# Five buffers for gathered U rows and three for gathered V rows in a product-key expert layer, in place of four and four

## The chip, the cores and the metric

The kernel runs on one core of a Trainium2 chip. The metric is device time in microseconds (us) from launch to end, the median of several executions. The profile is of one execution; its span is the time from the first instruction to the last.

## What is computed

One layer of a decoder for 1024 prompt tokens and 32 sample tokens (8 sequences of 4), model width 1024, all in float32: a modulated norm and one combined projection, sliding-window attention, a gated short convolution, the output projection, and then a feed-forward layer (PEER) that takes most of the time. Cut to that layer, the reference is:

```
q = (xb @ w_query)                      # 8 heads, 2 halves of 64
s = einsum('thcd,hcnd->thcn', q, keys)  # 128 keys in each half
sv, si = top_k(s, 16)                   # 16 best of each half
cv, ci = top_k(all 256 sums, 16)        # 16 best pairs
idx = i1 * 128 + i2                     # one of 16384 experts
g = softmax(cv)
a = gelu(einsum('thkd,td->thk', expert_u[idx], xb))
out = einsum('thk,thkd->td', g * a, expert_v[idx])
```

Each token has 8 heads with 16 experts each; each expert has one row of 1024 numbers (4 KB) in `expert_u` and one in `expert_v`.

## The kernel before, in words

The program has four stages that end in a barrier of all engines (modulation rows; attention of the prompt; attention of the sample; the first half of the convolution) and then the long last one, from about 1050 us to the end. It does the expert layer, and beside it the second half of the convolution's 80 weight blocks (`conv_steps`), the output projection and the queries of the later token tiles (`out_steps`).

The expert layer goes by *units*. A unit is one tile of 128 tokens and one head: 8 tiles by 8 heads are 64 units, and the sample tokens are 2 more, `UNITS` = 66. A unit has 16 steps `k`, one for each chosen expert of a token; `at = n * 16 + k` numbers the steps of all units, 0 to 1055. In each step:

- GpSimd (POOL) issues two indirect DMAs. `gather_u(n, k)` brings 128 rows of `expert_u`, one to each partition (512 KB), into a buffer of `u_ring`. `gather_v(n - 1, k)` does the same from `expert_v` for the unit before, into a buffer of `v_ring`. All 2112 go through one DMA queue, in the order U, V, U, V, and POOL does nothing else in this stage.
- VectorE (DVE) multiplies the U rows with the tokens and sums (`dot_rows`, L1247, "dot" below): one number for each token. A dot signals `dots_done`. Between the dots stand the top-16 searches for the next unit (`pick_half`, `pick_best`, `pick_key`, `pick_index`), which give the indices `idx` that the next unit's gathers wait for (`idx_made`, after the dot of k = 12).
- After the 16 dots of a unit ScalarE (ACT) takes the GELU, DVE multiplies by the gates (`weigh`, after the first dot of the next unit), and ACT makes a 128x128 diagonal matrix of the weights for each step (`make_diag`, eight buffers).
- TensorE (PE) multiplies the diagonal with the V rows (`add_row`, L1574, "block" below): two products of 128x512 in float32, four MATMUL rows in the trace, accumulated in two banks over the 128 steps of a tile. A block signals `rows_done`.

Each ring has `RING` = 4 buffers of 1024 words in each partition. U gather number `at` waits until the dot of number `at - 4` has released its buffer, V gather `at` until the block of number `at - 4` has:

```python
for n in range(UNITS + 1):
    if n < UNITS:
        pool.wait_ge(idx_made, n + 1)
    for k in range(TOPK):
        if n < UNITS:
            gather_u(n, k)
        if n:
            gather_v(n - 1, k)
```

Since POOL works in order, a V gather that waits for its buffer also holds back the U gathers behind it, and the reverse. At the end, for the last unit, only V gathers are left. After every 8 units DVE multiplies the summed banks out (`finish_y`), and PE's first block of the next tile waits for that.

Of the kernel before, what the change touches and what calls it, by code (L numbers as in the profile page):

```python
# [15 lines left out]
D = 1024  # L16
# [17 lines left out]
LOWEST = -3.0e38  # L34
PH, PK, TOPK = 8, 128, 16
UNITS = NT * PH + 2
RING = 4
DIAGS = 8
IDXS = 4
ABLK = 512  # L40
# [18 lines left out]
def build(nc, x_prompt, x_sample, cache_k, cache_v, state_conv, c_prompt, c_sample,  # L59
# [17 lines left out]
    eu = expert_u.rearrange("a n d -> (a n) d")  # L77
    ev = expert_v.rearrange("a n d -> (a n) d")
# [10 lines left out]
    with ctx:  # L89
# [3 lines left out]
        def sem(name):  # L93
            return ctx.enter_context(nc.semaphore(name))
# [19 lines left out]
        def row(names, at, *shape, dt=F32):  # L114
            n = 1
            for s in shape:
                n *= s
            n = (n + 7) // 8 * 8
            return [place(name, at + i * n, *shape, dt=dt) for i, name in enumerate(names)]
# [3 lines left out]
        def banks(a, n):  # L123
            return bank[:, a:a + n, :].rearrange("p a b -> p (a b)")
# [106 lines left out]
        def merged_T(j, k):  # L231
            if j < HT:
                return oT1[:, k, j * P:j * P + P]
            if j < NT:
# [1 line left out]
            return oT2[:, k, NP - NA:NBT]  # L236


        u_ring = row([f"u_ring{r}" for r in range(RING)], 0, D)
        v_ring = row([f"v_ring{r}" for r in range(RING)], 4096, D)  # L240
        h2b = row(["h2b0", "h2b1"], 8192, D)
        x2_now, y_now = row(["x2_now", "y_now"], 10240, D)
        prod = row(["prod0", "prod1"], 12288, D)
        G2 = place("G2", 14336, D)
        diag = row([f"diag{r}" for r in range(DIAGS)], 15360, P)
# [49 lines left out]
        q0_ps = sem("q0_in_psum")  # L295
        e_consts, e_keys_ps, e_keys_made, e_g2_in = (sem(n) for n in (
            "e_consts", "keys_in_psum", "keys_made", "g2_in"))
        u_in = [sem(f"u_in_{r}") for r in range(RING)]
        v_in = [sem(f"v_in_{r}") for r in range(RING)]
        q_in = [sem(f"q_in_{r}") for r in range(2)]  # L300
        dots_done, rows_done, s_ps, s_out, best_made, gate_exp, idx_made, gelu_made, wgt_made, diag_made = (
            sem(n) for n in ("dots_done", "rows_done", "s_in_psum", "s_out", "best_made", "gate_exp",
                             "idx_made", "gelu_made", "wgt_made", "diag_made"))
# [166 lines left out]
        @block.gpsimd  # L470
        def _(pool):
            link = Chain(pool, chain_pool)

            def where(view, pattern, base, mult, cmp, fill):
                link(pool.affine_select(out=view, in_=view, compare_op=cmp, fill=fill, base=base,
                                        pattern=pattern, channel_multiplier=mult))

            link(pool.memset(ident[:, :], 0.0))
            where(ident[:, :], [[-1, P]], 0, 1, ALU.not_equal, 1.0)
            link(pool.memset(sel_s[:, :], 0.0))  # L480
            for q in range(4):
                where(sel_s[:, :], [[-1, NS]], -NS * q, 1, ALU.not_equal, 1.0)
            link(pool.memset(eps[:, :], EPS))
            pool.sem_inc(consts_made, 1)
            barrier(pool, 0)

            link(pool.memset(maskt[:, :, :, :], 0.0))
            for m, own in ((0, 0), (1, 1), (2, 0)):
                where(maskt[:, m, own, :], [[-1, P]], 0, 1, ALU.is_ge, NEG)
                if m:  # L490
                    where(maskt[:, m, 1 - own, :], [[1, P]], -1, -1, ALU.is_ge, NEG)
            link(pool.memset(maskt[:, 0, 1, :], NEG))
            link(pool.memset(kpad[:, :, :, :, :], 0.0))
            link(pool.memset(vpad[:, :, :, :], 0.0))
            pool.sem_inc(attn_zeroed, 1)
            for t in range(NT):
                pool.wait_ge(qkv_out, t + 1)
                if t:
                    pool.wait_ge(pv_ps, t * 4)
                for half in range(2):  # L500
                    link(pool.tensor_copy(vpad[:, t % 2, :, 2 * HD * half:2 * HD * half + HD],  # L501
                                          qkv[:, D + KVW:QKV].rearrange("p (g d) -> p g d", g=NKV)))
                pool.sem_inc(v_placed, 1)
            barrier(pool, 1)

            link(pool.memset(s_mask[:, :], 0.0))
            link(pool.memset(qz[:, :, :, :, :], 0.0))
            cache = s_mask[0:NS, 0:NB * WIN].rearrange("p (b j) -> p b j", b=NB)
            new = s_mask[0:NS, NB * WIN:].rearrange("p (b l) -> p b l", b=NB)
            where(cache, [[-L, NB], [0, WIN]], 0, 1, ALU.is_ge, NEG)  # L510
            where(cache, [[L, NB], [0, WIN]], L - 1, -1, ALU.is_ge, NEG)
            where(cache, [[L, NB], [1, WIN]], -1, -1, ALU.is_ge, NEG)
            where(new, [[-L, NB], [0, L]], 0, 1, ALU.is_ge, NEG)
            where(new, [[L, NB], [0, L]], L - 1, -1, ALU.is_ge, NEG)
            where(new, [[-L, NB], [-1, L]], 0, 1, ALU.is_ge, NEG)
            pool.sem_inc(mask_s_made, 1)
            barrier(pool, 2)
            link(pool.iota(part_i[:, :], pattern=[[1, TOPK]], base=0, channel_multiplier=0))
            link(pool.tensor_copy(iota16[:, :], part_i[:, :]))
            link(pool.memset(keys_bd[:, :, :], 0.0))  # L520
            pool.sem_inc(e_consts, 1)
            barrier(pool, 3)

            def gather_u(n, k):
                at = n * TOPK + k
                if at >= RING:
                    pool.wait_ge(dots_done, at - RING + 1)
                pool.indirect_dma_start(out=u_ring[k % RING][:, :], out_offset=None, in_=eu,  # L528
                                        in_offset=bass.IndirectOffsetOnAxis(ap=idx[n % IDXS][:, k:k + 1], axis=0)
                                        ).then_inc(u_in[k % RING], 16)  # L530

            def gather_v(n, k):
                at = n * TOPK + k
                if at >= RING:
                    pool.wait_ge(rows_done, at - RING + 1)
                pool.indirect_dma_start(out=v_ring[k % RING][:, :], out_offset=None, in_=ev,  # L536
                                        in_offset=bass.IndirectOffsetOnAxis(ap=idx[n % IDXS][:, k:k + 1], axis=0)
                                        ).then_inc(v_in[k % RING], 16)

            for n in range(UNITS + 1):  # L540
                if n < UNITS:
# [6 lines that stand above are left out]
# [334 lines left out]
        def _(dve):  # L882
            link = Chain(dve, chain_dve)
            V = nc.vector
            w = dve.wait_ge
# [353 lines left out]

            def dot_rows(n, k):  # L1240
                at, t = n * TOPK + k, n // PH
                w(u_in[k % RING], 16 * (at // RING + 1))
                if at >= 2:
                    w(dots_done, at - 1)
                if at % (PH * TOPK) == 0 and t:
                    w(h2_in, 16 * t if t < NT else 16 * (NT + 3))
                V.tensor_tensor_reduce(out=prod[k % 2][:, :], in0=u_ring[k % RING][:, :],  # L1247
                                       in1=h2b[t % 2][:, :], scale=1.0, scalar=0.0, op0=ALU.mult,
                                       op1=ALU.add, accum_out=dot[n % 2][:, k:k + 1]).then_inc(dots_done, 1)

# [87 lines left out]
        def _(pe):  # L1338
            M, TR = nc.tensor.matmul, nc.tensor.transpose
            w = pe.wait_ge  # L1340
# [4 lines left out]
            for rows, n, at in ((c9, NB + 1, 0), (st16, NB * 2, 72), (cw4, 4, 200)):  # L1345
                for k in range(KC):
                    last = TR(small[:, at + k * n:at + (k + 1) * n], rows[0:n, k * P:(k + 1) * P], ident[0:n, 0:n])
            last.then_inc(small_ps, 1)
            pe.wait_ge(small_made, 1)
            for j in range(NBLK):  # L1350
                r = j % ARING
# [3 lines left out]
                for k in range(KC):  # L1355
                    last = M(banks(r, 1)[0:NB + 1, :], cT[:, k, :], ada_w[r][:, k, :], start=k == 0, stop=k == KC - 1)  # L1356
# [116 lines left out]
            for c in range(2):  # L1473
                for b in range(NB):
                    last = TR(banks(3 + 2 * c, 2)[:, b * P:(b + 1) * P], ck_sb[:, b, c * P:(c + 1) * P], ident[:, :])
# [90 lines left out]
            def add_row(n, k):  # L1566
                at, parts = n * TOPK + k, P if n < NT * PH else NS
                first, final = at % (PH * TOPK) == 0, (at + 1) % (PH * TOPK) == 0 or at + 1 == UNITS * TOPK
                if first and at:
                    w(y_read, n // PH)  # L1570
                w(v_in[k % RING], 16 * (at // RING + 1))
                w(diag_made, at + 1)
                for c in range(2):
                    last = M(banks(c, 1)[0:parts, :], diag[k % DIAGS][:, 0:parts], v_ring[k % RING][:, c * 512:(c + 1) * 512],  # L1574
                             start=first, stop=final)
                last.then_inc(rows_done, 1)

# [84 lines left out]
```

## Time and profile before

| | us |
|---|---|
| median of 3 runs | 4266.62 |
| lowest and highest of the runs | 4257.82, 4269.5 |
| the profiled execution's own time | 4249.22 |
| its span | 4247.4 |

| engine | busy us | share of the span |
|---|---|---|
| PE (matmul) | 3373.3 | 79% |
| DVE | 2463.8 | 58% |
| POOL | 2427.2 | 57% |
| ACT | 1004.3 | 24% |

The page reports 1259.02 MB moved by DMA, 1107.43 MB of them by the queue that POOL's gathers use. An issue of a gather counts as busy time of POOL, from its start until POOL can go on. "To landing" is the time from the start of that issue to the last of the 16 semaphore updates of the transfer. A released buffer shows as an idle time of POOL "<-PE bank L1574" (V) or "<-DVE dot L1247" (U) in front of a gather; 0.30 us of idle time stand in front of every gather, whether it waited or not.

### The profile page before, as it was taken

How to read it: one execution, taken by the hardware profiler on the slowest of the kernel's cores; microseconds unless marked ns; L12 is line 12 of the kernel's file. 1: busy time of each engine (PE TensorE's matmuls, PEld its weight loads, DVE VectorE, ACT ScalarE, POOL GpSimd, SP SyncE). 2: the span in 40 equal slices, each digit the busy share in tenths (PEclk: the TensorE clock that was granted, in tenths of full speed). 3: DMA queues.
4: the chain of work that ended last, by engine and by line, in shares of the span. 5: the costliest groups of instructions: out<-in, count | busy, mean ns of one | idle time of the engine just before them, and what ended most of it. 6: DMA issues, size and time to landing. Idle time of an engine off the chain costs nothing.

```text
span 4247.4 us, 35040 instructions
## 1 busy us (share of the span) xinstructions
PE 3373.3 (79%) x10326; PEld 1700.1 (40%) x10326; DVE 2463.8 (58%) x5652; ACT 1004.3 (24%) x2229; POOL 2427.2 (57%) x2160
## 2 busy tenths in 40 slices
PE   8577774997797899989998777776787677778777
PEld 1244443784443455545554332332242233223221
DVE  1244443344665677777676666666666666666663
ACT  0244442221122222222222221212121212222221
POOL 0000000001676777777776677777777777777776
PEclk9788896998899999999999999999999999999999
DMA  8100001643899999999999999999999999999998
GB/s 294 49 10 10 0 8 40 194 136 114 325 380 381 378 367 379 375 365 392 361 369 368 389 360 373 364 367 360 370 368 366 364 364 355 370 378 362 359 371 322
DMA packets 439469, 1259.02 MB, mean 296 GB/s; under 512 B 41209, under 2 KB 142265, under 8 KB 438696
## 3 DMA queue, kind: packets, MB, share of 16 engines
q0 software_dynamic: 304128, 1107.43, 69.3%
q1 hardware_dynamic: 114700, 131.24, 9.3%
q10 hardware_dynamic: 20454, 18.13, 1.4%
q8 instruction: 85, 1.39, 0.1%
q14 instruction: 102, 0.84, 0.1%
HBM read 1233.67 MB, written 25.00 MB: 296 GB/s over the span
## 4 chain that ended last, share of the span: by engine, by line
PE 35%; POOL 23%; DMA 23%; issue 10%; DVE 6%; ACT 2%; ACTq 0%; DVEq 0%; SPq 0%; POOLq 0%
DMA v_ring<-in_expert_v_dram,idx 19%; PE bank L1574 13%; POOL u_ring L528 12%; POOL v_ring L536 11%; PE bank L1503 7%; PE bank L1371 4%; DMA u_ring<-in_expert_u_dram,idx 3%; PE bank L1356 2%; PE bank L1530 2%; PE bank L1406 2%; PE bank L1549 1%; PE bank L1384 1%; DVE prod L1247 1%; PE bank L1392 1%; PE bank L1595 1%
## 5 line engine op out<-in xcount | busy, mean ns | idle before, releaser
L1574 PE MATMUL bank<-v_ring,diag 128*128 128x512 f32 (+1 forms) x4224 | 2079.9, 622 | 603.3 <-DMA v_ring<-in_expert_v_dram,idx 486.1
L1247 DVE CUSTOM_DVE_ANT_0 prod<-u_ring,h2b 128x1024 f32<-128x1024 f32 x1056 | 1288.5, 1226 | 972.6 <-DMA u_ring<-in_expert_u_dram,idx 884.9
L528 POOL DMA_INDIRECT u_ring<-in_expert_u_dram,idx x1056 | 1197.0, 1134 | 649.0 <-issue 307.4
L536 POOL DMA_INDIRECT v_ring<-in_expert_v_dram,idx x1056 | 1207.7, 1144 | 430.5 <-issue 228.0
L1574 PEld LDWEIGHTS bank<-v_ring,diag 128*128 128x128 f32 (+1 forms) x4224 | 744.2, 191 | 1758.2 <-DMA v_ring<-in_expert_v_dram,idx 1034.0
L810 ACT ACTIVATE diag<-ident,wgt 128x128 f32<-128x128 f32 x1024 | 352.5, 393 | 781.0 <-PE bank L1574 519.2
L1503 PE MATMUL bank<-hi,whi 128*128 128x512 f32 x640 | 315.7, 493 | 8.2 <-DVE wlo L1108 8.2
L501 POOL COPY vpad<-qkv 128x256 f32<-128x256 f32 x16 | 7.5, 467 | 459.1 <-PE bank L1406 420.1
L1503 PE MATMUL bank<-hi,wlo 128*128 128x512 f32 x640 | 251.7, 393 | 0.0
L1503 PE MATMUL bank<-lo,whi 128*128 128x512 f32 x640 | 251.6, 393 | 0.0
L802 ACT ACTIVATE act_dot<-dot 128x16 f32<-128x16 f32 x66 | 14.2, 216 | 816.8 <-DVE dot L1247 816.7
L1371 PE MATMUL bank<-w_qkv,hT 128*128 128x512 f32 x384 | 169.0, 597 | 1.1 <-ACTq L579 1.1
L1549 PEld LDWEIGHTS bank<-mT,wq_sb 128*128 128x128 f32 x1152 | 138.8, 192 | 30.7 <-issue 30.6
L711 ACT CAST whi<-wc 128x1024 fp32r<-128x1024 f32 x80 | 83.8, 1048 | 278.3 <-PE bank L1595 174.1
L1503 PEld LDWEIGHTS bank<-hi,whi 128*128 128x128 f32 x640 | 121.7, 190 | 65.1 <-issue 43.7
L1108 DVE TENSOR_TENSOR wlo<-wc,whi 128x1024 fp32r<-128x1024 f32 x80 | 98.0, 1225 | 82.5 <-ACT whi L711 78.4
L1503 PEld LDWEIGHTS bank<-lo,whi 128*128 128x128 f32 x640 | 121.8, 190 | 56.1 <-issue 36.2
L1530 PE MATMUL bank<-wo_sb,oT 128*128 128x512 f32 (+1 forms) x288 | 136.7, 606 | 8.5 <-ACTq L769 6.0
L1549 PE MATMUL bank<-mT,wq_sb 128*128 128x128 f32 (+1 forms) x1152 | 138.5, 274 | 0.0
L1503 PEld LDWEIGHTS bank<-hi,wlo 128*128 128x128 f32 x640 | 120.9, 189 | 27.1
L1406 PE MATMUL bank<-pT,vpad 128*128 128x128 f32 x512 | 80.8, 324 | 48.1 <-issue 32.9
L1371 PEld LDWEIGHTS bank<-w_qkv,hT 128*128 128x128 f32 x384 | 73.0, 192 | 90.5 <-issue 88.8
(223 smaller groups left out, 2663.5 us busy)
## 6 DMA issues: line engine op xcount, KB each, us to landing
wc<-in_w_in_dram SPq DMA_DIRECT2D x80, 512.0 KB, 7.7
ada_w<-in_w_ada_dram SPq DMA_DIRECT2D x12, 2048.0 KB, 8.0
u_ring<-in_expert_u_dram,idx POOLq DMA_INDIRECT x1056, 6.5
v_ring<-in_expert_v_dram,idx POOLq DMA_INDIRECT x1056, 6.5
wo_sb<-in_w_out_dram SPq DMA_DIRECT2D x2, 4096.0 KB, 18.8
wq_sb<-in_w_query_dram SPq DMA_DIRECT2D x2, 4096.0 KB, 19.3
w_qkv<-in_w_in_dram SPq DMA_DIRECT2D x1, 6144.0 KB, 22.9
q_st<-q_dh ACTq DMA_DIRECT2D x65, 64.0 KB, 5.4
```

Of the source, the lines that this page charges most:

```text
L528: pool.indirect_dma_start(out=u_ring[k % RING][:, :], out_offset=None, in_=eu, in_offset=bass.IndirectOffsetOnAxis(ap=idx[n % IDXS][:, k:k ...
L536: pool.indirect_dma_start(out=v_ring[k % RING][:, :], out_offset=None, in_=ev, in_offset=bass.IndirectOffsetOnAxis(ap=idx[n % IDXS][:, k:k ...
L810: nc.scalar.activation(diag[k % DIAGS][:, 0:parts], base[:, :], ACT.Copy, scale=wgt[n % 2][:, k:k + 1]).then_inc(diag_made, 1)
L1108: V.tensor_tensor(wlo[b % 2][:, :, :], wc[b % WRING][:, :, :], whi[b % 2][:, :, :].bitcast(F32), ALU.subtract).then_inc(w_split, 1)
L1247: V.tensor_tensor_reduce(out=prod[k % 2][:, :], in0=u_ring[k % RING][:, :], in1=h2b[t % 2][:, :], scale=1.0, scalar=0.0, op0=ALU.mult, op1 ...
L1356: last = M(banks(r, 1)[0:NB + 1, :], cT[:, k, :], ada_w[r][:, k, :], start=k == 0, stop=k == KC - 1)
L1371: last = M(banks(c, 1), hT(t)[:, k, :], w_qkv[:, k, c * 512:(c + 1) * 512], start=k == 0, stop=k == KC - 1)
L1406: last = M(banks(7, 1)[:, at:at + P], vpad[:, s, g, HD * e:HD * e + P], pT[:, s, 2 * pair + e, :], start=e == 0 and s == 0, stop=e == 1 an ...
L1503: last = M(at, (wlo if part == 2 else whi)[b % 2][:, k, :], (lo if part == 1 else hi)[:, k, 0:NA], start=(k, part) == (0, 0), stop=(k, par ...
L1530: last = M(banks(2 + c, 1)[0:parts, :], merged_T(j, k), wo_sb[:, k, c * 512:(c + 1) * 512], start=k == 0, stop=k == KC - 1)
L1549: last = M(banks(2, 2)[:, h * P:h * P + parts], wq_sb[:, k, h * P:(h + 1) * P], mT[:, k, 0:parts], start=k == 0, stop=k == KC - 1)
L1574: last = M(banks(c, 1)[0:parts, :], diag[k % DIAGS][:, 0:parts], v_ring[k % RING][:, c * 512:(c + 1) * 512], start=first, stop=final)
```

## The change

`RING` is replaced by `URING` = 5 and `VRING` = 3. The eight buffers take the same 8192 words in each partition: U the first 5120, V the next 3072. U gather `at` now waits for the dot of number `at - 5`, V gather `at` for the block of number `at - 3`. The buffer and its semaphore are picked by `at` modulo the ring's size, where `k` modulo 4 did it before. Each engine's instructions stay the same in kind, number and order.

```diff
-RING = 4
+URING, VRING = 5, 3
...
-        u_ring = row([f"u_ring{r}" for r in range(RING)], 0, D)
-        v_ring = row([f"v_ring{r}" for r in range(RING)], 4096, D)
+        u_ring = row([f"u_ring{r}" for r in range(URING)], 0, D)
+        v_ring = row([f"v_ring{r}" for r in range(VRING)], URING * D, D)
...
             def gather_u(n, k):
                 at = n * TOPK + k
-                if at >= RING:
-                    pool.wait_ge(dots_done, at - RING + 1)
-                pool.indirect_dma_start(out=u_ring[k % RING][:, :], out_offset=None, in_=eu,
+                if at >= URING:
+                    pool.wait_ge(dots_done, at - URING + 1)
+                pool.indirect_dma_start(out=u_ring[at % URING][:, :], out_offset=None, in_=eu,
...
             def gather_v(n, k):
                 at = n * TOPK + k
-                if at >= RING:
-                    pool.wait_ge(rows_done, at - RING + 1)
-                pool.indirect_dma_start(out=v_ring[k % RING][:, :], out_offset=None, in_=ev,
+                if at >= VRING:
+                    pool.wait_ge(rows_done, at - VRING + 1)
+                pool.indirect_dma_start(out=v_ring[at % VRING][:, :], out_offset=None, in_=ev,
...
-                w(u_in[k % RING], 16 * (at // RING + 1))
+                w(u_in[at % URING], 16 * (at // URING + 1))
...
-                w(v_in[k % RING], 16 * (at // RING + 1))
+                w(v_in[at % VRING], 16 * (at // VRING + 1))
```

## Rows read from the trace of the kernel before

**Rows 1.** The page's chain that ended last: shares by engine, then by line.

```profile
PE 35%; POOL 23%; DMA 23%; issue 10%; DVE 6%; ACT 2%; ACTq 0%; DVEq 0%; SPq 0%; POOLq 0%
DMA v_ring<-in_expert_v_dram,idx 19%; PE bank L1574 13%; POOL u_ring L528 12%; POOL v_ring L536 11%; PE bank L1503 7%; PE bank L1371 4%; DMA u_ring<-in_expert_u_dram,idx 3%; PE bank L1356 2%; PE bank L1530 2%; PE bank L1406 2%; PE bank L1549 1%; PE bank L1384 1%; DVE prod L1247 1%; PE bank L1392 1%; PE bank L1595 1%
```

**Rows 2.** Busy time by stretch of the last stage; the first line names the columns.

```profile
core 0: us, PE busy (x) PEld busy (x) DVE busy (x) ACT busy (x) POOL busy (x), PEclk, DMA share, GB/s
1067.00:1260.00 193.00, 167.78 (x576) 89.94 (x577) 121.06 (x291) 42.41 (x93) 137.37 (x122) 0.93 0.95 352
1260.00:2230.00 970.00, 874.11 (x2894) 485.30 (x2894) 676.43 (x1611) 246.82 (x523) 727.29 (x631) 0.99 1.00 374
2230.00:4205.00 1975.00, 1502.32 (x3738) 612.90 (x3736) 1251.49 (x3049) 400.98 (x950) 1505.11 (x1328) 0.98 0.98 367
4205.00:4242.00 37.00, 34.10 (x77) 7.50 (x76) 3.43 (x7) 4.59 (x17) 15.69 (x17) 1.00 0.80 269
```

**Rows 3.** Timeline, DVE and POOL: start us, us, instruction, idle before, releaser.

```profile
3006.16 1.23 DVE L1247 CUSTOM_DVE_ANT_0 prod<-u_ring,h2b 128x1024 f32<-128x1024 f32 x1 [1.01 <-DMA u_ring<-in_expert_u_dram,idx]
3006.26 1.94 POOL L536 DMA_INDIRECT v_ring<-in_expert_v_dram,idx  x1 [0.30 <-issue]
...
3055.09 0.94 POOL L536 DMA_INDIRECT v_ring<-in_expert_v_dram,idx  x1 [0.30 <-issue]
3056.33 0.93 POOL L528 DMA_INDIRECT u_ring<-in_expert_u_dram,idx  x1 [0.30 <-issue]
3057.57 0.94 POOL L536 DMA_INDIRECT v_ring<-in_expert_v_dram,idx  x1 [0.30 <-issue]
```

**Rows 4.** V gathers of 1067 to 1260, 1260 to 2230, 2230 to 4205 us.

```profile
L536 POOL DMA_INDIRECT v_ring<-in_expert_v_dram,idx x61: 932/945/1967, 1067.4 to 1258.1; - x61
DMA to landing us min/median/max: 4.5/6.4/10.6
...
L536 POOL DMA_INDIRECT v_ring<-in_expert_v_dram,idx x315: 932/940/1979, 1261.2 to 2227.6; - x158
DMA to landing us min/median/max: 4.8/7.2/19.5
...
L536 POOL DMA_INDIRECT v_ring<-in_expert_v_dram,idx x664: 932/941/1979, 2230.5 to 4204.3; - x166
DMA to landing us min/median/max: 4.5/6.3/18.3
```

**Rows 5.** Waits of POOL in the same three stretches: us in total, times, longest.

```profile
POOL v_ring L536 <- PE bank L1574: 20.4, 20, 8.8
POOL u_ring L528 <- DVE dot L1247: 5.1, 3, 2.2
...
POOL v_ring L536 <- PE bank L1574: 48.4, 68, 8.1
POOL u_ring L528 <- DVE dot L1247: 21.6, 15, 4.2
...
POOL v_ring L536 <- PE bank L1574: 118.4, 221, 4.0
POOL u_ring L528 <- DVE dot L1247: 17.0, 18, 1.6
```

**Rows 6.** Timeline, first and last V gather counted, block third before each.

```profile
1077.90 3.75 PE L1574 MATMUL bank<-v_ring,diag 128*128 128x512 f32 x4 [23.52 <-ACT diag L810]
1078.28 1.63 POOL L536 DMA_INDIRECT v_ring<-in_expert_v_dram,idx  x1 [0.31 <-issue]
...
4203.31 1.90 PE L1574 MATMUL bank<-v_ring,diag 128*32 128x512 f32 x4 [0.65 <-DMA v_ring<-in_expert_v_dram,idx]
4204.34 0.94 POOL L536 DMA_INDIRECT v_ring<-in_expert_v_dram,idx  x1 [0.30 <-issue]
```

**Rows 7.** The last unit, 4205 to 4242 us: V gathers alone.

```profile
DMA to landing us min/median/max: 4.8/5.2/6.6
...
4205.59 1.01 POOL L536 DMA_INDIRECT v_ring<-in_expert_v_dram,idx  x1 [0.30 <-PE bank L1574]
4235.13 0.94 POOL L536 DMA_INDIRECT v_ring<-in_expert_v_dram,idx  x1 [0.78 <-PE bank L1574]
```

More of the change, by code:

```diff
@@ L297, in build @@
             "e_consts", "keys_in_psum", "keys_made", "g2_in"))
-        u_in = [sem(f"u_in_{r}") for r in range(RING)]
-        v_in = [sem(f"v_in_{r}") for r in range(RING)]
+        u_in = [sem(f"u_in_{r}") for r in range(URING)]
+        v_in = [sem(f"v_in_{r}") for r in range(VRING)]
         q_in = [sem(f"q_in_{r}") for r in range(2)]
@@ L525, in gather_u @@
                 at = n * TOPK + k
-                if at >= RING:
-                    pool.wait_ge(dots_done, at - RING + 1)
-                pool.indirect_dma_start(out=u_ring[k % RING][:, :], out_offset=None, in_=eu,
+                if at >= URING:
+                    pool.wait_ge(dots_done, at - URING + 1)
+                pool.indirect_dma_start(out=u_ring[at % URING][:, :], out_offset=None, in_=eu,
                                         in_offset=bass.IndirectOffsetOnAxis(ap=idx[n % IDXS][:, k:k + 1], axis=0)
-                                        ).then_inc(u_in[k % RING], 16)
+                                        ).then_inc(u_in[at % URING], 16)
             def gather_v(n, k):
                 at = n * TOPK + k
-                if at >= RING:
-                    pool.wait_ge(rows_done, at - RING + 1)
-                pool.indirect_dma_start(out=v_ring[k % RING][:, :], out_offset=None, in_=ev,
+                if at >= VRING:
+                    pool.wait_ge(rows_done, at - VRING + 1)
+                pool.indirect_dma_start(out=v_ring[at % VRING][:, :], out_offset=None, in_=ev,
                                         in_offset=bass.IndirectOffsetOnAxis(ap=idx[n % IDXS][:, k:k + 1], axis=0)
-                                        ).then_inc(v_in[k % RING], 16)
+                                        ).then_inc(v_in[at % VRING], 16)
             for n in range(UNITS + 1):
@@ L1246, in dot_rows @@
                     w(h2_in, 16 * t if t < NT else 16 * (NT + 3))
-                V.tensor_tensor_reduce(out=prod[k % 2][:, :], in0=u_ring[k % RING][:, :],
+                V.tensor_tensor_reduce(out=prod[k % 2][:, :], in0=u_ring[at % URING][:, :],
                                        in1=h2b[t % 2][:, :], scale=1.0, scalar=0.0, op0=ALU.mult,
@@ L1570, in add_row @@
                     w(y_read, n // PH)
-                w(v_in[k % RING], 16 * (at // RING + 1))
+                w(v_in[at % VRING], 16 * (at // VRING + 1))
                 w(diag_made, at + 1)
                 for c in range(2):
-                    last = M(banks(c, 1)[0:parts, :], diag[k % DIAGS][:, 0:parts], v_ring[k % RING][:, c * 512:(c + 1) * 512],
+                    last = M(banks(c, 1)[0:parts, :], diag[k % DIAGS][:, 0:parts], v_ring[at % VRING][:, c * 512:(c + 1) * 512],
                              start=first, stop=final)
```

## The prediction

> **What bounds the kernel now.** I read the chain that ended last first. It names no single engine: V gathers in flight, the blocks that use them, and POOL's issues of both kinds of gather follow one another, 55% of the span between them [rows 1]. That is a loop through a buffer. Then busy time by stretch [rows 2]. From 1260 to 4205 us the DMA engines are busy 0.98 to 1.00 of the time at 367 to 374 GB/s. POOL is nearly full too: in the long stretch 1505.11 us of busy time and 1328 times the 0.30 us that stand before every gather make 1904 of 1975 us. The waits of POOL tell how little the rings hold it back [rows 5]: in that stretch V gathers waited 118.4 us in 221 cases, 52 us without the 0.30 us of each, U gathers 17.0 us in 18 cases. So today the DMA engines and POOL's issuing set the pace together, and four buffers of each kind are just enough to keep both going. One step takes 1975 / 664 = 2.97 us there and 970 / 315 = 3.08 us from 1260 to 2230 us [rows 2, 4]. When nothing disturbs it, POOL could issue a pair every 2.48 us [rows 3].
>
> **The change, part by part.** No instruction is added. Only two waits move.
>
> *The V side.* A V buffer's cycle is 0.30 us from release to issue, the time to landing, and the block of 1.90 us [rows 6]. With the median landing that is 0.30 + 6.3 + 1.90 = 8.5 us in the long stretch and 0.30 + 7.2 + 1.90 = 9.4 us in the one before [rows 4]. Four buffers gave it 4 x 2.97 = 11.9 and 4 x 3.08 = 12.3 us. Three give 8.9 and 9.2 us. The median gather just fits in the long stretch and just doesn't in the other. What costs time is the gathers over the median and the blocks that PE starts late, since it has convolution, projection and score products between them.
>
> I took each V gather's issue and the end of the block third before it, which will release its buffer after the change. The first of them started at 1078.28 us, and its block ended at 1077.90 + 3.75 = 1081.65: it would have had to wait 3.6 us more, with 0.28 us from release to issue. The last started at 4204.34 with its block ending at 4205.21: 1.1 us more [rows 6]. Of the 1040 V gathers between 1067 and 4205 us, 714 were issued before that moment. The lateness sums to 121 us over the first 61, 484 us over the 315 of the next stretch and 546 us over the 664 of the long one, 1151 us together.
>
> How much becomes time? Not the sum itself. When POOL stops for a V gather, all later gathers shift with it, and so the next two gathers don't have that wait again; the blocks that release them are old enough not to shift. Each wait counts three times in my sum, so the high end is 1151 / 3 = 384 us, if every gather takes as long to land as before. The low end is nothing: a stop of POOL lets the queue in front of the DMA engines drain, and gathers then land sooner. The rows have a stretch where the queue is short. In the last unit V gathers go alone, DMA is at 0.80, and they land in 5.2 us [rows 2, 7]. I take that as what a gather needs without a queue, so the cushions are 6.4 - 5.2 = 1.2 us in the first stretch, 7.2 - 5.2 = 2.0 in the second, 6.3 - 5.2 = 1.1 in the long one [rows 4, 7]. Only lateness above the cushion leaves DMA engines idle. Summed over the same gathers it is 64, 87 and 224 us, 375 together, and a third of it is **+125 us**. This is the value I take; 0 and 384 stay as its ends.
>
> The Trainium skill, "DMA: Bandwidth & Descriptors", section on the anatomy of one DMA, speaks against a loss of this size: it fits 2.0 us plus the bytes over 436 GB/s to a single DMA from GpSimd, an estimate of 3.2 us for 512 KB. With 3.2 us in place of 5.2 the cushions would be 3.2, 4.0 and 3.1 us, the lateness above them 11 + 15 + 42 = 68 us, and the term +23 us. No gather in these stretches landed in under 4.5 us, so the rows decide.
>
> *The last unit.* Its V gathers already wait for the ring each time: 15 intervals in 4235.13 - 4205.59 = 29.54 us, 1.97 us each, a four-buffer cycle of 7.9 us [rows 7]. Three buffers make 2.63 us of it, 15 x 0.66 = **+10 us**. Nothing covers this; both ends are close, since here all terms of the cycle stay.
>
> *The U side.* With a fifth buffer the waits of U gathers for a dot should go: 5.1 + 21.6 + 17.0 = 43.7 us in 36 cases, 33 us beyond the 0.30 us of each [rows 5]. While they lasted the DMA engines had a queue, so I count a third, as for V: **-11 us**, ends 0 and -33. The rest of the fifth buffer buys nothing. POOL reaches each U gather after the V gather in front of it, and that one is now the later. At a unit's start the fifth buffer also frees too early: its dot is number k = 11, but the indices come after the dot of k = 12.
>
> *POOL's issue time* is not fixed. It is 0.94 us in the median and up to 1.98 [rows 4]; the long ones start while a dot is running, and those are 1.23 us long [rows 3]. Moved issues may meet more or fewer dots. I price that at nothing, with 1.04 us for each issue that changes sides as the unit of the error; 40 net changes would be 40 us either way, part of the range.
>
> The sum is 125 + 10 - 11 = **+124 us**. Against the profiled execution it is 4249.2 + 124 = 4373 us. That execution is 17 us below the median of the runs, so I forecast 4266.6 + 124 = **4391 us**, 2.9% slower.
>
> **The rivals.**
>
> *Hidden by the DMA engines, no change.* The DMA share is 0.98 to 1.00 and the bytes are the same. The mean lateness for each gather is 484 / 315 = 1.5 and 546 / 664 = 0.8 us, each under its cushion of 2.0 and 1.1. If lateness were even, the V term would be 0, the sum 10 - 11, and the time 4266 us. Against it: it is not even, the longest landing is 18.3 to 19.5 us [rows 4] and 221 ring waits show up in a ring that is 3.4 us longer than the median cycle [rows 5]. Chance 0.07. The same Trainium skill page, in its section on bandwidth, would make this the outcome, since it puts the limit of HBM transfers at about 358 GB/s per core: a kernel at that limit doesn't feel its rings. The rows run at 367 and 374 GB/s over long stretches, above it.
>
> *Faster.* The U ring is the one that matters: its 33 us of waits go whole, and the V side costs only its last unit. That gives 4266.6 - 33 + 10 = 4244 us. It needs V gathers to land in under 3 x 2.97 - 2.20 = 6.7 us in the long stretch and 3 x 3.08 - 2.20 = 7.0 us in the other nearly always. The second median is already 7.2. Chance 0.03.
>
> *No cushion.* The landing time is transfer and reply, not queue; a drained queue shortens nothing. Then the V term is 384 us and the time 4266.6 + 384 + 10 - 11 = 4650 us. For it: gathers under 5 us are rare. Against it: the last unit's 5.2 us. Chance 0.06.
>
> *The change isn't there.* The rings could be so placed that U and V still meet as before. The waits in the diff say otherwise; it has no chance worth naming.
>
> **How the numbers follow.** The forecast has 0.84, the rivals 0.07, 0.03 and 0.06. A measurement of this kernel can tell about 0.3%, 13 us, from no change. Within the forecast the V term may be off by half of itself, because the cushion rests on one row and a third is the share only if lateness is spread evenly: +62 to about +190 us, with 10 - 11 and some 20 us for POOL's issue times around it. That is 4310 to 4480 us, and it leaves out the rivals and the forecast's own tails, 2 in 10. Faster gets the 0.03, no change its 0.07 and 0.01 of the forecast's lower tail, slower the rest.
>
> **What would show it.** V gathers waiting for PE should rise from 187 us [rows 5] in the three stretches to several hundred, with most gathers among them. U gathers should hardly wait for dots. Landing medians should fall, to between 5.2 and 6.0 us in the long stretch. The DMA share should drop to about 0.95 with the GB/s. POOL's busy time should stay near 2400 us. The last unit should take about 10 us more. I'd be wrong in kind if the V waits rose and the DMA share stayed at 0.98 (the first rival), wrong in size if landing stayed at 6.3 us and the time went past 4500 (the third).

## The result and the profile after

| | before, us | after, us |
|---|---|---|
| median | 4266.65 | 4488.28 |
| lowest, highest | 4257.82, 4269.5 | 4471.43, 4496.09 |
| profiled execution, its span | 4249.22, 4247.4 | 4486.26, 4484.4 |

The ratio is 1.0518, with a 95% interval of 1.0484 to 1.0552: the change costs 222 us, where I had forecast 124 and a range up to 4480. The sign and the place were right, and the size was not. One of six executions of the run v3_fill_one, further down, took 8309.75 us; its ratio leaves that one out, its median counts it.

The chain that ended last answers to [rows 1]. V gathers in flight rose from 19 to 28%, and POOL's two issues fell from 23 to 15%:

```profile
PE 38%; DMA 31%; POOL 15%; issue 7%; DVE 5%; ACT 2%; ACTq 0%; DVEq 0%; SPq 0%; POOLq 0%
DMA v_ring<-in_expert_v_dram,idx 28%; PE bank L1574 16%; POOL u_ring L528 8%; POOL v_ring L536 7%; PE bank L1503 7%; PE bank L1371 4%; DMA u_ring<-in_expert_u_dram,idx 2%; PE bank L1356 2%; PE bank L1406 1%; PE bank L1530 1%; PE bank L1549 1%; PE bank L1595 1%; PE bank L1384 1%; PE bank L1392 1%; DVE prod L1247 1%
```

The busy time by stretch answers to [rows 2]. The stretches are cut at the same gathers as there: V gathers 0 to 60, 61 to 375, 376 to 1039, and the last 16.

```profile
1071.50:1278.80 207.30, 171.44 (x578) 89.48 (x578) 123.31 (x293) 42.52 (x93) 132.59 (x122) 0.94 0.91 330
1278.80:2340.40 1061.60, 899.42 (x2894) 493.24 (x2894) 676.19 (x1610) 247.29 (x523) 704.93 (x631) 0.96 0.94 341
2340.40:4437.00 2096.60, 1537.53 (x3738) 621.65 (x3738) 1253.49 (x3049) 401.72 (x950) 1490.59 (x1327) 0.96 0.95 346
4437.00:4479.40 42.40, 33.90 (x72) 6.58 (x72) 1.75 (x5) 4.59 (x17) 15.35 (x16) 1.00 0.67 215
```

Cut at those gathers, the four stretches took 193.8, 969.3, 1975.1 and 36.8 us before. They grew by 13, 92, 122 and 6 us, which with 4 us ahead of them is the whole difference of the spans. Nothing is lost elsewhere. The DMA share fell to 0.94 and 0.95 and the bytes in a second with it, from 374 and 367 to 341 and 346 GB/s. TensorE's granted clock fell too, from 0.99 and 0.98 to 0.96 in both long stretches.

POOL's waits in the first three stretches answer to [rows 5]:

```profile
POOL v_ring L536 <- PE bank L1574: 44.2, 29, 10.9
...
POOL v_ring L536 <- PE bank L1574: 211.5, 157, 11.8
...
POOL v_ring L536 <- PE bank L1574: 302.8, 342, 5.7
```

V gathers waited 558.5 us in 528 cases, against 187.2 us in 309 before. Without the 0.30 us of each that is 400 us against 94. No row of a U gather that waits for a dot is left, where there were 33 us net. POOL's busy time went down by 43 us, from 2427.2 to 2383.9. 306 - 33 - 43 = 230 us accounts for nearly all of the 237 us between the spans. That is POOL's own time line added up: it says where the time appears, not yet why.

The landing times answer to [rows 4], in the same three stretches, and the last row to [rows 7]:

```profile
DMA to landing us min/median/max: 4.1/6.2/9.0
...
DMA to landing us min/median/max: 4.1/6.2/17.4
...
DMA to landing us min/median/max: 4.0/6.1/14.1
...
DMA to landing us min/median/max: 4.1/5.0/5.4
```

This is where my forecast went wrong. I had let the medians of 6.4, 7.2 and 6.3 us sink to 5.2 before any of it cost time. They sank to 6.2, 6.2 and 6.1.

The timeline of POOL shows how. It stands still for 5.43 us, then issues eight gathers, with 9.3 us from the first start to the last and most intervals at 1.24 us, then stands still again for 2.71 us:

```profile
3202.93 0.93 POOL L536 DMA_INDIRECT v_ring<-in_expert_v_dram,idx  x1 [5.43 <-PE bank L1574]
3204.17 0.94 POOL L528 DMA_INDIRECT u_ring<-in_expert_u_dram,idx  x1 [0.30 <-issue]
...
3212.20 0.94 POOL L528 DMA_INDIRECT u_ring<-in_expert_u_dram,idx  x1 [0.30 <-issue]
3215.85 0.93 POOL L536 DMA_INDIRECT v_ring<-in_expert_v_dram,idx  x1 [2.71 <-PE bank L1574]
```

A burst at 1.24 us a gather fills the queue again, since the packets of one gather take 1.44 us of each DMA engine's time (128 packets of 4 KB at 179 ns in the mean and 16 small ones, spread over 16 engines). Of the 979 V gathers from number 61 to 1039, some 650 were issued without a stop of more than 0.1 us in front of them and landed in 6.2 us in the median; the 53 that followed a stop of over 2 us landed in 5.1 us. The 0.30 us that stands before every gather is not counted in these stops.

### The profile page after: what moved, and what is told of

It reads as the page before. It is cut to its first block, busy times and chain, and to the rows that moved or that the text cites. A ratio compares the mean times of both kernels' runs of the same rounds, so it can differ in the third digit from the quotient of the medians.

```text
span 4484.4 us, 35040 instructions
## 1 busy us (share of the span) xinstructions
PE 3442.6 (77%) x10326; PEld 1719.5 (38%) x10326; DVE 2466.2 (55%) x5652; ACT 1005.6 (22%) x2229; POOL 2383.9 (53%) x2160
## 4 chain that ended last, share of the span: by engine, by line
PE 38%; DMA 31%; POOL 15%; issue 7%; DVE 5%; ACT 2%; ACTq 0%; DVEq 0%; SPq 0%; POOLq 0%
DMA v_ring<-in_expert_v_dram,idx 28%; PE bank L1574 16%; POOL u_ring L528 8%; POOL v_ring L536 7%; PE bank L1503 7%; PE bank L1371 4%; DMA u_ring<-in_expert_u_dram,idx 2%; PE bank L1356 2%; PE bank L1406 1%; PE bank L1530 1%; PE bank L1549 1%; PE bank L1595 1%; PE bank L1384 1%; PE bank L1392 1%; DVE prod L1247 1%
## 5 line engine op out<-in xcount | busy, mean ns | idle before, releaser
L1574 PE MATMUL bank<-v_ring,diag 128*128 128x512 f32 (+1 forms) x4224 | 2133.8, 634 | 771.0 <-DMA v_ring<-in_expert_v_dram,idx 658.9
L536 POOL DMA_INDIRECT v_ring<-in_expert_v_dram,idx x1056 | 1163.3, 1102 | 739.9 <-PE bank L1574 581.0
```

Source lines behind the costliest of these rows:

```text
L536: pool.indirect_dma_start(out=v_ring[at % VRING][:, :], out_offset=None, in_=ev, in_offset=bass.IndirectOffsetOnAxis(ap=idx[n % IDXS][:, k ...
```

## The experiments

Three theories could explain the size, beside the one that the V buffer's cycle is the bound (theory A): the new places of the buffers in memory (B), a fifth U buffer that lets U crowd V out of the queue (C), and TensorE's lower clock (D). The first runs take the change apart. The times of the kernel before that stand with them are its medians on the same chip; the ratios are the measured ratios of the runs and can differ a little from the quotient of the two medians.

**Three V buffers alone.**

```diff
-URING, VRING = 5, 3
+URING, VRING = 4, 3
```

> Four U buffers and three V buffers, placed as before the change (U from word 0, V from word 4096), one buffer fewer in all. Theory A (the loss is the cycle of the V buffer: with three buffers a step can't be shorter than a third of release, landing, block and lateness): the same loss as the change, 4488 us, or up to 15 us more since the fifth U buffer did next to nothing. Rival B (placement: the V buffers now lie from word 5120 and the buffer no longer follows k, and the packets got longer from 173 to 179 ns): V lies where it lay before, so most of the 222 us should be gone, under 4350 us. Rival C (the fifth U buffer lets POOL run ahead with U and crowd the V gathers out of the queue): clearly faster than the change, 4400 us or less.

Measured 4475.36 us against 4264.83, ratio 1.0519 (1.0482 to 1.0557). The two medians alone give 1.0494, so the loss is 211 us by the medians and 221 by the ratio; either way it is that of the change within the noise. The whole loss comes from going from four V buffers to three. V lies at its old place here, so placement has no part that can be told, and beside three V buffers no effect of the fifth U buffer can be told either. The waits in its long stretch are those of the change:

```profile
POOL v_ring L536 <- PE bank L1574: 295.4, 349, 5.4
```

**Five U buffers with four V.** For nine buffers the ninth lies in words that the last stage leaves free:

```diff
-URING, VRING = 5, 3
+URING, VRING = 5, 4
...
-        u_ring = row([f"u_ring{r}" for r in range(URING)], 0, D)
-        v_ring = row([f"v_ring{r}" for r in range(VRING)], URING * D, D)
+        SLOTS = [r * D for r in range(8)] + [42496]
+        u_ring = [place(f"u_ring{r}", SLOTS[r], D) for r in range(URING)]
+        v_ring = [place(f"v_ring{r}", SLOTS[URING + r], D) for r in range(VRING)]
```

> Five U buffers and four V buffers, a ninth buffer in words that the last stage leaves free. Theory A: the time of the kernel before within 0.3%, 4255 to 4267 us, with U waits gone. Rival C (more U buffers hurt V): slower than 4280 us. Rival B (at % 5 and V from word 5120): slower too, 4350 us or more.

Measured 4253.75 us against 4264.83, ratio 0.9975 (0.995 to 1.0). My U term of -11 us has the right size, at the edge of what can be told.

**Five V buffers with four U.** The same, with 4 and 5.

> The ninth buffer given to V instead. If V is the side on which the loop is tight even with four buffers (V waits 94 us net, U waits 33 us), this gains a little: 4240 to 4262 us. If the DMA engines at 0.98 hold the time, no difference that can be told, 4255 to 4275 us.

Measured 4233.21 us, ratio 0.9933 (0.9901 to 0.9964), 32 us faster than before by the medians and 7 us under the nearer of my two ranges. The fifth buffer is worth more on the V side than on the U side, 32 against 11 us. So four V buffers were not quite enough to keep the DMA engines going.

**The mirror: three U, five V.**

```diff
-URING, VRING = 5, 3
+URING, VRING = 3, 5
```

> The mirror of the change: three U buffers, five V buffers. A U buffer's cycle is 0.3 us, a landing of 6.3 us and a dot of 1.23 us, 0.7 us shorter than V's. Theory A with that cycle: slower than before, but by less than the change, 4350 to 4440 us. If the rule is that any ring of three loses the same, 4488 us.

Measured 4408.82 us, ratio 1.0352 (1.0325 to 1.0379): 144 us lost in place of 222. A ring of three is too short for U as well, and by less, in keeping with its shorter cycle. The 80 us between the two kernels are not the cycle's alone: the mirror also has a fifth V buffer, worth 32 us beside four U buffers, and the change a fifth U buffer. No run has three U and four V.

**Half a block, three V buffers and four.** The second 512 columns of each V row's product are left out, and the gathers stay whole.

```diff
-                for c in range(2):
+                for c in range(1):
                     last = M(banks(c, 1)[0:parts, :], diag[k % DIAGS][:, 0:parts], ...
```

> The change (5 U, 3 V), but each block does only the first 512 columns: the second half of every V row's product is left out, the gathers stay whole. The block drops from 1.96 to 0.98 us. Theory A (time is a third of the V buffer's cycle): 0.98 us off the cycle is 0.33 us off each step, at most 340 us over 1040 steps, until the DMA engines and POOL bound it again at about the pace of four buffers: 4200 to 4290 us. If instead the longer time is in the transfers themselves (packets 179 in place of 173 ns) and the block is not on the path, it stays above 4430 us.

> The same halved block with four U and four V buffers (the second half of every V row's product is left out). Theory A: with four buffers the block is hardly on the path, so little comes off: 4190 to 4250 us. If PE as such bounded the kernel before, 1000 us less PE work would show as 100 us or more: under 4160 us.

Measured 4382.05 us with three V buffers and 4245.82 with four, against 4268.35. Less PE work took 106 us off the one and 23 us off the other. So the block is on the path with three V buffers and hardly with four, as theory A has it, but the first figure misses its 4200 to 4290. Two rows of the long stretch of the three-buffer run, its busy times by the columns of [rows 2] and its products, say why:

```profile
2299.00:4331.00 2032.00, 1391.89 (x2412) 472.56 (x2410) 1253.21 (x3049) 400.11 (x950) 1468.09 (x1328) 0.65 0.97 357
...
L1574 PE MATMUL bank<-v_ring,diag x1330: 591/1061/1223, 2298.7 to 4329.9; 128*128 128x512 f32 x186, 128*32 128x512 f32 x4
```

The median product took 1061 ns in place of 592, at a granted clock of 0.65 in that stretch: TensorE went back and forth between its two levels, 1.2 and 2.4 GHz, and about seven in ten products took over 1000 ns. With half of each block's products left out TensorE did 2412 products in the stretch, where it did 3738 with the change, and its clock fell from 0.96. So the block shrank from 2.07 to 1.78 us there and not to 0.98. The step in that stretch fell from 3.16 to 3.06 us, 0.10, and a third of the 0.29 us is 0.10. In the stretch before, the block shrank by 0.67 us and the step by only 0.09, where a third would be 0.22. The mean landing rose by 0.25 us there, from 6.50 to 6.75, which took part of it back. The DMA share of 0.97 is a likely cause of the rest, not tested.

**No U gathers after the first few, three V buffers and four.** All later dots read the same U rows, so what U brings is left out and V is alone in the queue.

```diff
-                    if n < UNITS:
+                    if n * TOPK + k < URING:
                         gather_u(n, k)
...
-                w(u_in[at % URING], 16 * (at // URING + 1))
+                if at < URING:
+                    w(u_in[at % URING], 16 * (at // URING + 1))
```

> The change with only the first five U gathers; all later dots read those same rows, so what U brings is left out, and V gathers are alone in the queue for the whole stage. It measures what a V gather needs to land without a queue. Theory A1 (my cushion was read from the last unit, where V is alone, and 5.2 us holds only for that): landing median 5.0 to 5.3 us here, while with U between them it can't fall under about 6.1. Step about (0.3 + 5.1 + 1.96) / 3 = 2.45 us plus lateness, time 3700 to 3880 us. Rival A2 (the last unit was special, a V gather needs 6 us anyway): landing 6.0 us or more, step 2.75 us and more, time over 3950 us.

> Four U and four V buffers with only the first four U gathers; later dots read the same rows, so what U brings is left out. V alone, four buffers. With three and no U the step was 2.71 to 2.97 us and 84 to 89% of V gathers waited for their buffer. Theory A: with four the cycle of about 8.1 us gives 2.0 us a step, so PE's own work (2.0 us of block and 0.44 us of the rest) bounds it: step 2.45 to 2.65 us, waits still frequent because nothing else holds POOL, time 3720 to 3900 us. If three buffers were not what bounded that kernel: 3980 us or more.

Measured 4030.7 us with three V buffers and 3690.22 with four. In a queue of V alone going from four V buffers to three costs 340 us, more than in the real kernel. The long stretch of the run with three, by columns as in [rows 2], and its V gathers:

```profile
2188.00:3986.00 1798.00, 1479.63 (x3739) 615.54 (x3738) 1223.47 (x3047) 414.00 (x957) 784.25 (x664) 0.98 0.69 210
...
DMA to landing us min/median/max: 4.0/5.1/10.2
POOL v_ring L536 <- PE bank L1575: 990.5, 640, 8.0
```

The landing of 5.1 us confirms that the last unit was no exception; alone, a V gather needs that long. The time of 4030.7 missed my 3700 to 3880 and lies where the rival A2 had it, but A2's landing of 6.0 us or more did not come. I had added lateness only in words. The step in the long stretch came out at 2.71 us, and the measured parts give (0.30 + 5.18 + 0.60 + 2.00) / 3 = 2.69: release, mean landing, lateness of the block, block. With four buffers 3690 us lies just under the expected range, and its step of 2.32 us under the 2.45 to 2.65 that PE's own work was to allow.

**Half the U rows.** Each later U gather brings 64 rows, to partitions 0 to 63; what it would bring to the others is left out.

```diff
-                pool.indirect_dma_start(out=u_ring[at % URING][:, :], out_offset=None, in_=eu,
-                                        in_offset=bass.IndirectOffsetOnAxis(ap=idx[n % IDXS][:, k:k + 1], axis=0)
+                few = P if at < URING else P // 2
+                pool.indirect_dma_start(out=u_ring[at % URING][0:few, :], out_offset=None, in_=eu,
+                                        in_offset=bass.IndirectOffsetOnAxis(ap=idx[n % IDXS][0:few, k:k + 1], axis=0)
```

> The change, but each U gather after the first five brings 64 rows in place of 128 (the other 64 partitions keep the old rows, so what they would bring is left out): the same number of gathers in the same order, half the U bytes in front of each V gather. Theory A1 (what a V gather needs to land is its own 5.15 us plus the work of the U gather in front of it): landing about halfway between 5.15 with no U and 6.2 with full U, 5.5 to 5.8 us, step 2.75 to 2.95 us, time 4060 to 4260 us. If it is the presence of a gather on POOL and in the queue and not its bytes, landing stays over 6.0 us and the time over 4350 us.

Measured 4750.99 us: slower by 263 us than the change, with fewer bytes. Both ranges missed. The long stretch:

```profile
2450.00:4707.00 2257.00, 1547.48 (x3739) 618.63 (x3738) 1253.92 (x3049) 401.99 (x950) 1398.07 (x1327) 0.96 0.96 245
...
DMA to landing us min/median/max: 4.0/7.4/15.1
```

The DMA share is 0.96 at only 245 GB/s. The packets of 4 KB took 256 ns in the mean, against 179 with the change. Packets carry no name of their gather; told apart by their order they took about 300 ns in U gathers and 230 in V gathers, an estimate. So this run isn't the halved load that I wanted. It tests the cycle from the other side all the same: mean landing went up by 1.0 us, and the step from 3.16 to 3.40 us, with (0.30 + 7.23 + 0.29 + 2.07) / 3 = 3.30 from its parts. The Trainium skill, "SBUF — State Buffer", section on the DMA port swizzle, says that partitions 0 to 63 reach no more of the DMA's ports than 0 to 31 do, so that a tile of 64 partitions has half the ports of one of 128. The longer packets agree with that; that it is the ports was not tested.

**Six U, two V buffers.**

> Six U buffers, two V buffers: one step further. Theory A: a step is half of the V buffer's cycle, (0.3 + landing + 0.3 + 2.0) / 2. With stops before nearly every V gather the queue is short for V, but one U gather still lies in front: landing 5.2 to 5.6 us, step 3.9 to 4.1 us, time 5200 to 5400 us. Rival (the cushion keeps growing with the stops until V lands as if alone in an idle queue, 4.5 us): step 3.55, under 4900 us. Rival (no cushion at all, landing stays 6.2 us): step 4.4, over 5600 us.

Measured 5457.52 us, ratio 1.2796 (1.2743 to 1.285). Long stretch:

```profile
2667.00:5402.00 2735.00, 1772.26 (x3739) 680.66 (x3737) 1254.68 (x3050) 404.60 (x951) 1444.89 (x1327) 0.88 0.79 266
...
DMA to landing us min/median/max: 4.0/5.3/11.8
```

This run refutes what I had written as theory A1, that a V gather with U between can't land in under about 6.1 us. It lands in 5.3. But it does so at a DMA share of 0.79 and a step of 4.12 us: the short landing is bought with idle DMA engines. The time is over my range by 58 us. I had counted a block of 2.0 us; PE's clock fell to 0.88 in the long stretch and the mean block rose to 2.39 us.

The parts of the cycle in us, each a mean over the same 664 V gathers in the long stretch, with "late" for the time from landing to the start of the block. The cycle is their sum and 0.30 us of release. The last column counts the V gathers whose issue began within about 0.30 us of the end of the block that freed their buffer:

| kernel | DMA share | landing | late | block | cycle / V buffers | step | V gathers issued at once on release |
|---|---|---|---|---|---|---|---|
| before, 4 V | 0.98 | 6.67 | 0.51 | 2.02 | 2.38 | 2.97 | 8% |
| the change, 3 V | 0.95 | 6.22 | 0.37 | 2.07 | 2.99 | 3.16 | 42% |
| half the U rows, 3 V | 0.96 | 7.23 | 0.29 | 2.07 | 3.30 | 3.40 | 70% |
| no U, 3 V | 0.69 | 5.18 | 0.60 | 2.00 | 2.69 | 2.71 | 89% |
| no U, 4 V | 0.75 | 5.53 | 1.36 | 1.96 | 2.29 | 2.32 | 71% |
| 2 V | 0.79 | 5.31 | 0.20 | 2.39 | 4.10 | 4.12 | 88% |

The cycle over the number of buffers is a floor under the step. Where most gathers are issued on release, the step lies within 0.1 us of it. That nearness is bookkeeping and no test, since the parts are measured on the same gathers; the test is that leaving out a buffer or part of a block moved the time. The change lies between: 0.17 us above its floor, with a ring that binds in 42% of the steps. What sets the pace in the other steps, POOL or the DMA engines, no run tells apart.

**TensorE's clock.** Small products into an unused bank, ahead of PE's wait for each V gather; two of them, then one, then one with four V buffers:

```diff
+                for _ in range(2):
+                    M(banks(7, 1)[:, 0:P], ident[:, :], ident[:, :], start=True, stop=True)
                 w(v_in[at % VRING], 16 * (at // VRING + 1))
```

> The change plus two small products into a bank that nothing uses, ahead of PE's wait for each V gather: they fill PE's pauses, 0.55 us a step. Theory D (part of the loss is TensorE's clock, granted 0.96 where it was 0.98 to 0.99, with 82 blocks over 2.3 us where there were 41): the granted clock rises above 0.98, slow blocks fall under 40, and the time falls by 15 to 60 us to about 4430 to 4470 us. If the clock has no part: no faster than the change, or slower by what of the 0.55 us lands on late blocks, up to 4560 us.

> The change plus one small product into an unused bank ahead of each V wait, 0.27 us in PE's pauses. Two of them raised the granted clock from 0.96 to 0.98 but cost 23 us. Theory D (the lower clock is a real part of the loss, hidden there by the cost of the filling): clock above 0.97 and a time 5 to 30 us below the change's 4488. If the clock is only a symptom of the longer pauses, worth at most a third of 0.05 us a block: 4480 to 4505 us.

> The same small product with four and four buffers: what filling costs where the V buffer's cycle is not the bound. Theory A: 4255 to 4280 us, no difference that can be told, since four buffers cover 0.27 us of lateness. If filling costs here what it costs with three buffers, 4275 us or more.

Measured 4511.63 us with two, 4488.73 with one, and 4290.11 with one and four V buffers, ratio 1.0072 (1.005 to 1.0095). In the long stretch the clock went from 0.96 to 0.98 with two and 0.97 with one. Filling didn't make the change faster, so the clock is not a large part of the loss. But it cost 24 us with four V buffers and nothing that can be told with three, though three should feel 0.27 us of PE work more. The 4290 us also missed the 4255 to 4280 that theory A had for four buffers, so these don't cover the added work whole. With three, something of about that size may have been given back. It agrees with the clock's arithmetic: the block was 0.06 us longer in the second stretch and 0.05 in the long one, a third of which over 979 steps is 17 us. I hold about 20 of the 222 us for the clock's, and count that as argued and not shown. It is hardly more than the noise of the change's own time, 15 us either way.

**Five and five.** The tenth buffer stands in the second half of the product buffers, whose contents nobody reads and which are bf16 here. The last run changes only the type of the product buffers, with four and four.

```diff
-        prod = row(["prod0", "prod1"], 12288, D)
+        prod = [place(f"prod{r}", 12288 + 512 * r, D, dt=BF16) for r in range(2)]
+        SLOTS = [r * D for r in range(8)] + [42496, 13312]
```

> Five and five, ten buffers: the ninth in free words, the tenth where the second product buffer was, whose contents nobody reads and which is now two of bf16. Five V buffers gave 0.67% and five U buffers 0.25% each alone. If the waits were separate the two add: 4220 to 4230 us, 0.9% below before. If the DMA engines at 0.98 to 1.00 are what is left: no better than five V buffers, 4230 to 4245 us. A dot that is slower with a bf16 output would show as over 1.23 us.

> Four and four buffers, the product buffers that nobody reads in bf16, as in the kernel with five and five. If the gain of that kernel (66 us, where five V gave 32 and five U 11) is due to the buffers alone, this is no faster than before: 4255 to 4275 us. If the narrower writes of the dots take something off, 4235 to 4250 us.

Measured 4203.74 us against 4269.76, ratio 0.9848 (0.9806 to 0.9891), for five and five; 4268.23 against 4266.02, ratio 1.0 (0.998 to 1.002), for the type alone. So the gain of 66 us is the buffers'. It beats both kernels and lies under both of my ranges, 4220 to 4230 and 4230 to 4245 us. By the medians it is more than the 43 us of the two single buffers together, but the intervals of the three runs are too wide to tell. One of the two expectations was that a DMA share of 0.98 to 1.00 leaves nothing more to win. It does leave something: the second stretch takes 944.7 us in place of 969.3.

## Why the prediction was wrong in size

**What bounds the kernel: right in the main.** The waits, the lower DMA share of 0.95 and the chain all came where the steps put them, and the run with three V and four U buffers lost the same. That four buffers of each kind were "just enough" was not: five V buffers took 32 us off, and five of each 66.

**The lateness: right, and the share of a third somewhat high.** If the 1151 us are cut by what the landing medians really gave up, 0.2, 1.0 and 0.2 us, the lateness above that is 111, 237 and 474 us over the same gathers. A third of the 822 is 274 us. The run with four U and three V buffers lost 211 us by its medians, about 7 of them in the last unit, so its V term is 204 us, a quarter of the 822. The share of a third thus made up for some of the error of the next step, and that was luck.

**The cushion: this is the step that failed.** I wrote that with a landing of 5.2 us "what a gather needs without a queue", the cushions are 1.2, 2.0 and 1.1 us, and that "only lateness above the cushion leaves DMA engines idle". The first half is right, as the run without U gathers shows. The second is not. The row of 5.2 us came from a stretch with a DMA share of 0.80 [rows 2, 7]. The run with two V buffers shows the price of such a landing in full: 5.3 us at a share of 0.79. In the table no kernel lands its V gathers in under 6.2 us in the mean at a DMA share of 0.95 or more. The queue drains only while a stop lasts and is refilled by the burst behind it, and most gathers are in the burst. The V term measured 204 us (214 by the ratio), where I took 125 between 0 and 384. That the short stops and the bursts keep the landing at 6.1 us is read from the trace of the change; no run changes the bursts alone.

**The last unit: right in kind, +6 us against +10.** Its landing fell from 5.2 to 5.0 us. I had written that all terms of the cycle stay.

**The U side: right in size where it can show**, -11 us with four V buffers. With three the fifth U buffer gave nothing that can be told.

**POOL's issue time: 43 us less**, at the edge of the 40 I allowed. V gathers started less often inside a dot, 528 times in place of 561, and a V issue took 1102 ns in the mean against 1144. The gain disappeared in the stops.

**The clock: not in the forecast.** It fell from 0.99 and 0.98 to 0.96 as PE's pauses grew, and the longer blocks lie on the V cycle. How much of the loss is its own stays open.

**The rivals.** No change, and faster, were rightly small. The third, no cushion, was taken as all or nothing. The truth lies between it and the forecast, and my range stopped 8 us short of it. Of the signs, the landing in the long stretch, 6.1 us, came just above my 5.2 to 6.0, and the V waits rose to 528 of 1041, half and not most.

## What to carry to other kernels

The floor that a ring puts under a step is its whole cycle over the number of buffers: release, landing, how late the consumer is, and the consumer's own time. Take the landing time from a stretch that runs at the DMA share you want to keep, never from a quieter one, and compare means and the tail with the pace, since a median that just fits is already a loss. With unequal consumers the buffer belongs to the side with the longer cycle, here V, and a share of 0.98 doesn't prove that a further buffer is worthless.

## What the runs showed of the hardware that I had not expected

- A 64-row gather is not half a gather. With 64 partitions written in place of 128 by every second gather, the mean 4 KB packet took 256 ns in place of 179, so 245 GB/s filled the engines to 0.96.
- The mean packet was longer in the runs in which the DMA engines had less to do. In the long stretch a 4 KB packet of the gathers took 174 ns on average before, 179 with the change, 194 with two V buffers and 216 with V alone. The median stayed at 159 in all four; what grows is the share of packets over 300 ns, from 3 to 4, 8 and 13%. So the DMA share overstates the load: V alone counts 0.69 at 210 GB/s, where 0.98 went with 367.
- An indirect DMA's issue that begins while a dot is running ends 0.81 us after the dot's end, in the median of 1005 such issues before, and 84% of those that begin over 0.05 us into the dot end within 0.01 us of that. One that begins before the dot keeps its 0.94 us in the median. In [rows 3] the dot ends at 3007.39 and the issue at 3008.20.
- Halving the product work of each step lowered TensorE's granted clock from 0.96 to 0.65 in the long stretch, and the median product went from 592 to 1061 ns. The block came down by 0.29 us, where half of its 2.07 us would be 1.03.
